# Joined gate and up matmuls: a copy moved ahead of a high part on ScalarE, an add moved ahead of a low part on VectorE

## The chip, the cores and the metric

The kernel runs on one core of a Trainium2 chip, in one launch. The metric is the device time of the whole program in microseconds (us). The kernel before takes 2538.83 us, the median of three runs (2538.58 to 2539.39).

## The reference

Two transformer blocks, one behind the other, over 512 tokens of width 1024 in float32. The change touches only the four gated nets ("nets 0 to 3") of the first block, two in each of its two layers:

```python
def swiglu(h, w_gate, w_up, w_down):
    return (jax.nn.silu(h @ w_gate) * (h @ w_up)) @ w_down

for l in range(DEPTH):                                   # DEPTH = 2
    x = x + 0.5 * swiglu(rms_norm(x, ffn1_norm[l]), ffn1_wg[l], ffn1_wu[l], ffn1_wd[l])
    ...                                                  # attention and short convolution
    x = x + 0.5 * swiglu(rms_norm(x, ffn2_norm[l]), ffn2_wg[l], ffn2_wu[l], ffn2_wd[l])
```

The hidden width is 2816, which is 22 tiles of 128. The second block (convolution, latent attention, cross attention, an MLP of width 4096) is not touched.

## The kernel before

**Split numbers.** Matmuls are made in float32r. Each operand is held as a high part (a rounded copy, made by ScalarE: `..._hi`) and a low part (the rest, made by VectorE as value minus high part: `..._lo`).

**Activations and weights.** Weights come from HBM through a ring of four slots of `raw` (SyncE's queue), 8 tiles of 128x128 to a slot.

**The nets.** Each net takes its 22 hidden tiles in two ways. The first 6 (net 0) or 4 (nets 1 to 3) go in pairs (`pair`): gate and up product apart. The others, 16 or 18 to a net and 70 in all, go one to a window (`fast_window`), where gate and up product of a tile are joined in a scheme of sums (seven products where the plain one has eight): 7 calls of `terms`, each of 4 pairs of matmuls (128x512 and 128x256 columns), write into `bank[0]`, `psT` and `bank[1]`. Partial results are copied out of `bank[0]` three and a half times by ScalarE (L1695, L1704, L1708, L1717) and added by VectorE (L2423, L2433, L2439, L2448, L2450). Two more additions are done by accumulating DMAs that GpSimd issues (L3345 into `tmp[0]`, L3348 into `tmp[2]`). VectorE scales both (L2442, L2453), ScalarE takes the silu (L1723), VectorE multiplies (L2456), and the hidden tile is split (`hidden_hi` L1687, `hidden_lo` L2410).

**Side products.** Between these calls TensorE multiplies tiles of an earlier group of hidden tiles with down weights into `psS` (`side(w, 0)` and `side(w, 1)`, 3 to 5 tiles each, 3 matmuls a tile); `side_adds` adds finished chunks to `x`. The low parts of these down weights are made by `whole_hi` (ScalarE writes the high part and the negated raw value's copy, L1629 and L1630) and another accumulating DMA of GpSimd (`side_lo`, L3337).

**Weights of the next window.** While window w runs, VectorE and ScalarE make those of window w+1: `corner_hi` and `corner_lo` (`cwh`, `cwl`), `weight_sums` (L2322, L2325, L2327), `sums_hi` and `sums_lo` in two halves (L1622, L2333), `last_hi` and `last_lo` (L1637, L2338).

**What sets the order.** All orders are written out by hand: each engine does its own list in that order, and semaphores hold it where it needs another. SyncE's queue loads, for each window, gate weights (L579), up weights (L579), and two units of down weights (L603, one or two pieces each). The gate slot and the second down slot come free at the end of `weight_sums`, the up slot and the first down slot at the end of `last_lo`. The down loads also wait for the accumulating DMA that read their slot before. The order of each engine's list inside `fast_window` is what is changed. TensorE's list (`fast_window` at L921) stays; its waits `k_sn` are ScalarE's copies, `k_ev` VectorE's adds, `k_lo` VectorE's low parts. GpSimd's list is

```python
pool.wait_ge(k_ev, 5 * g + 1)                    # L2423
pool.dma_start(tmp[0][:, 0:QT], tmp[1][:, 0:QT], accum_op=ALU.add).then_inc(k_fd[0], 16)
side_lo(g, 1, net.side_cols(w, 1))               # waits for whole_hi(w, 1)
pool.wait_ge(k_ev, 5 * g + 2)                    # L2433
pool.dma_start(tmp[2][:, QT:S], tmp[3][:, QT:S], accum_op=ALU.add).then_inc(k_fd[1], 16)
```

Of the kernel before, what the change touches and what calls it, by code (L numbers as in the profile page):

```python
# [40 lines left out]
def build(nc, t, out):  # L41
# [75 lines left out]
    with ctx:  # L117
# [217 lines left out]
        s_h = sem("hidden_ready")  # L335
# [1239 lines left out]
        def _(act):  # L1575
# [22 lines left out]
            def ffn(c0, q0, N, nf):  # L1598
# [25 lines left out]
                def whole_hi(j, i):  # L1624
                    c = c0 + 4 * (PLAIN + j)
                    landing(c + 2 + i)
                    act.wait_ge(s_used, q0 + c - RING + 2 + 2 * i)
                    a, b_, n = (2 * i + 1) * UNIT, (2 + i) * UNIT, side_cols(j, i)
                    act.activation(whi[:, a:a + n], raw[:, b_:b_ + n], ACT.Copy).then_inc(s_hi, 1)  # L1629
                    act.activation(wlo[:, a:a + n], raw[:, b_:b_ + n], ACT.Copy, scale=-1.0).then_inc(k_nh, 1)  # L1630
# [53 lines left out]
                def hidden_hi(w):  # L1684
                    tile = 2 * PLAIN + w
                    act.wait_ge(s_h, fb + tile + 1)
                    act.activation(chunk(hhi, tile % HT), tmp[3 if w < 0 else 2][:, :], ACT.Copy).then_inc(s_hh, 1)  # L1687

                def fast_window(w):
                    u, g, f = 4 * (PLAIN + w), G0 + w, fb + 2 * PLAIN + w  # L1690
                    on = w + 1 < FAST
                    act.wait_ge(k_pe, 5 * g + 1)
                    if g:
                        act.wait_ge(k_ev, 5 * g - 4)
                    act.activation(part[0][:, :], bank[0][:, :], ACT.Copy).then_inc(k_sn, 1)  # L1695
                    if w == 0:
                        hidden_hi(-1)
                    whole_hi(w, 1)
                    if on:
                        corner_hi(w + 1)  # L1700
                    act.wait_ge(k_pe, 5 * g + 3)
                    if g:
                        act.wait_ge(k_ev, 5 * g)
                    act.activation(part[2][:, :], bank[0][:, :], ACT.Copy).then_inc(k_sn, 1)  # L1704
                    act.wait_ge(k_pe, 5 * g + 4)
                    if g:
                        act.wait_ge(k_ev, 5 * g - 2)
                    act.activation(part[1][:, :], bank[0][:, :], ACT.Copy).then_inc(k_sn, 1)  # L1708
                    if on:
                        sums_hi(w + 1, 0)  # L1710
                        whole_hi(w + 1, 0)
                    else:
                        ahead(u + 4)
                        ahead(u + 5)
                    act.wait_ge(s_used, q0 + c0 + u + 3)
                    act.wait_ge(k_ev, 5 * g + 2)
                    act.activation(part[1][:, 0:QT], bank[0][:, QT:S], ACT.Copy).then_inc(k_sn, 1)  # L1717
                    if on:
                        sums_hi(w + 1, 1)
                    else:  # L1720
                        ahead(u + 6)
                    act.wait_ge(s_gs, f + 1)
                    act.activation(tmp[0][:, :], tmp[0][:, :], ACT.Silu).then_inc(s_si, 1)  # L1723
                    if on:
                        last_hi(w + 1)
                    hidden_hi(w)

                for w in range(PLAIN):
                    pair(w)
                for w in range(FAST):  # L1730
                    fast_window(w)
                for m in range(KC):
                    ahead(LAST_AT + m + AHEAD)
                    x_hi(N + 1, m)
                    if m == 0:
                        act.activation(acc[:, :], chunk(x, m), ACT.Square).then_inc(s_sq, 1)
                        continue
                    if m > 2:
                        act.wait_ge(s_sq, (N + 1) * KC + m - 1)
                    act.activation(tmp[m % 2][:, :], chunk(x, m), ACT.Square).then_inc(s_sqm, 1)  # L1740
# [523 lines left out]
        def _(dve):  # L2264
# [35 lines left out]
            def ffn(c0, q0, N, nf):  # L2300
# [29 lines left out]
                def sums_lo(j, i):  # L2330
                    dve.wait_ge(s_hi, q0 + c0 + 4 * (PLAIN + j) + 1 + 2 * i)
                    a = 2 * i * UNIT
                    dve.tensor_tensor(wlo[:, a:a + UNIT], tw[:, i * UNIT:(i + 1) * UNIT], whi[:, a:a + UNIT].bitcast(F32),  # L2333
                                      ALU.subtract).then_inc(k_lo, 1)
# [5 lines left out]
                def ahead(u):  # L2340
                    if u == 4 * PLAIN:
                        sums_lo(0, 0)
                    elif u == 4 * PLAIN + 1:
                        pass
                    elif u == 4 * PLAIN + 2:
                        sums_lo(0, 1)
                        last_lo(0)
                    else:
                        split(c0 + u, q0, UNIT_TILES.get(u, 8), 2 if u == LAST_AT else 1)
# [49 lines left out]
                def side_adds(w, i):  # L2399
                    ends = side_ends(w, i)  # L2400
                    if ends:
                        dve.wait_ge(s_used, q0 + c0 + 4 * (PLAIN + w) + 2 + 2 * i)
                    for grp, m in ends:
                        dve.scalar_tensor_tensor(chunk(x, m), psS[:, m % 2 * S:(m % 2 + 1) * S], 0.5, chunk(x, m), ALU.mult,
                                                 ALU.add).then_inc(k_xa, 1)
# [7 lines left out]
                def fast_window(w):  # L2413
                    u, g, f = 4 * (PLAIN + w), G0 + w, fb + 2 * PLAIN + w
                    c = q0 + c0 + u
                    on = w + 1 < FAST
                    t1, t2 = quarter
                    split1 = lambda j, t: folds(tmps[:, j * S:(j + 2) * S])[:, :, t]
                    if w:
                        side_adds(w - 1, 1)  # L2420
                    dve.wait_ge(k_pe, 5 * g + 2)
                    dve.wait_ge(k_sn, 4 * g + 1)
                    dve.tensor_tensor(split1(0, t1), folds(psT[:, 0:S]), folds(part[0][:, :]), ALU.add).then_inc(k_ev, 1)  # L2423
                    if on:
                        corner_lo(w + 1)
                        weight_sums(w + 1)
                        sums_lo(w + 1, 0)
                    else:
                        ahead(u + 4)
                    dve.wait_ge(k_pe, 5 * g + 4)  # L2430
                    dve.wait_ge(k_sn, 4 * g + 3)
                    dve.wait_ge(s_hl, f)
                    dve.tensor_tensor(split1(2, t2), folds(bank[1][:, :]), folds(part[1][:, :]), ALU.add).then_inc(k_ev, 1)  # L2433
                    side_adds(w, 0)
                    if not on:
                        ahead(u + 5)
                    dve.wait_ge(s_used, c + 3)
                    dve.wait_ge(k_sn, 4 * g + 4)
                    dve.tensor_tensor(tmp[0][:, t2], bank[0][:, 0:QT], part[1][:, t1], ALU.add).then_inc(k_ev, 1)  # L2439
                    dve.wait_ge(k_ev, 5 * g + 3)  # L2440
                    dve.wait_ge(k_fd[0], 16 * (g + 1))
                    dve.tensor_tensor(tmp[0][:, :], tmp[0][:, :], inv[:, :], ALU.mult).then_inc(s_gs, 1)  # L2442
                    if on:
                        sums_lo(w + 1, 1)
                    else:
                        ahead(u + 6)
                    dve.wait_ge(k_pe, 5 * g + 5)
                    dve.tensor_tensor(part[2][:, :], bank[1][:, :], part[2][:, :], ALU.add).then_inc(k_ev, 1)  # L2448
                    dve.wait_ge(k_ev, 5 * g + 4)
                    dve.tensor_tensor(tmp[2][:, t1], part[2][:, t1], part[2][:, t2], ALU.add).then_inc(k_ev, 1)  # L2450
                    dve.wait_ge(k_ev, 5 * g + 5)
                    dve.wait_ge(k_fd[1], 16 * (g + 1))
                    dve.tensor_tensor(tmp[2][:, :], tmp[2][:, :], inv[:, :], ALU.mult).then_inc(s_us, 1)  # L2453
                    dve.wait_ge(s_us, f + 1)
                    dve.wait_ge(s_si, f + 1)
                    dve.tensor_tensor(tmp[2][:, :], tmp[2][:, :], tmp[0][:, :], ALU.mult).then_inc(s_h, 1)  # L2456
                    if on:
                        last_lo(w + 1)
                    hidden_lo(w)

                for w in range(PLAIN):
                    pair(w)
                for w in range(FAST):
                    fast_window(w)
                side_adds(FAST - 1, 1)
                for m in range(KC):
                    ahead(LAST_AT + m + AHEAD)
# [973 lines left out]
```

## Time and profile before

| | |
|---|---|
| median of three runs | 2538.83 us |
| profiled execution, its own time | 2540.39 us |
| its span, first to last instruction | 2538.5 us |
| TensorE matmul busy | 2496.1 us (98%) |
| VectorE busy | 2021.7 us (80%) |
| ScalarE busy | 1371.9 us (54%) |
| GpSimd busy | 551.5 us (22%) |
| granted TensorE clock | 1.000 |

The profile is of one execution. PE is TensorE, DVE VectorE, ACT ScalarE, POOL GpSimd, SP SyncE. Times in a row are from the start of the span. The end of a matmul is modelled, so the distance from the start of one to the start of the next says more than its duration. The windows lie from 79 to 333 us (net 0), 577 to 850 (net 1), 932 to 1205 (net 2) and 1454 to 1730 (net 3).

### The profile page before, as it was taken

How to read it: one execution, taken by the hardware profiler on the slowest of the kernel's cores; microseconds unless marked ns; L12 is line 12 of the kernel's file. 1: busy time of each engine (PE TensorE's matmuls, PEld its weight loads, DVE VectorE, ACT ScalarE, POOL GpSimd, SP SyncE). 2: the span in 40 equal slices, each digit the busy share in tenths (PEclk: the TensorE clock that was granted, in tenths of full speed). 3: DMA queues.
4: the chain of work that ended last, by engine and by line, in shares of the span. 5: the costliest groups of instructions: out<-in, count | busy, mean ns of one | idle time of the engine just before them, and what ended most of it. 6: DMA issues, size and time to landing. Idle time of an engine off the chain costs nothing.

```text
span 2538.5 us, 33440 instructions
## 1 busy us (share of the span) xinstructions
PE 2496.1 (98%) x12252; PEld 2079.6 (82%) x12252; DVE 2021.7 (80%) x2760; ACT 1371.9 (54%) x2185; POOL 551.5 (22%) x530
## 2 busy tenths in 40 slices
PE   9999999999999999999999999999999999999999
PEld 7888888888878888888888878788888888888887
DVE  7788877778888688888677788886899787788873
ACT  5555545446555465555454555554578535655442
POOL 4122201322222002222023122221078322100002
PEclk9999999999999999999999999999999999999999
DMA  5566642235656536666422266665333333333331
GB/s 158 132 148 148 144 114 86 80 90 134 144 139 149 135 89 147 142 152 148 113 67 87 84 141 139 142 150 142 96 79 77 118 98 108 87 102 105 101 104 58
DMA packets 527608, 296.99 MB, mean 117 GB/s; under 512 B 46801, under 2 KB 516566, under 8 KB 527190
## 3 DMA queue, kind: packets, MB, share of 16 engines
q1 hardware_dynamic: 486674, 244.19, 33.3%
q0 software_dynamic: 40320, 50.35, 12.0%
q8 instruction: 98, 1.61, 0.3%
q14 instruction: 64, 0.52, 0.1%
q10 hardware_dynamic: 452, 0.32, 0.0%
HBM read 240.27 MB, written 4.19 MB: 96 GB/s over the span
## 4 chain that ended last, share of the span: by engine, by line
PE 68%; DVE 14%; DMA 8%; ACT 5%; issue 4%; POOL 0%; DVEq 0%; ACTq 0%
PE bank L893 6%; PE bank L776 6%; PE bank L777 6%; PE bank L778 6%; DMA raw<-in_ffn_wu 5%; DMA tmps<-tmps 3%; PE bank L894 3%; PE bank L1455 3%; DVE tw L2322 2%; PE psT L958 2%; PE psT L959 2%; PE psT L960 2%; ACT whi L1622 2%; PE psS L914 2%; PE psS L916 2%
## 5 line engine op out<-in xcount | busy, mean ns | idle before, releaser
L2269 DVE TENSOR_TENSOR wlo<-raw,whi 128x1024 fp32r<-128x1024 f32 (+2 forms) x212 | 288.9, 1364 | 51.7 <-ACT whi L1582 48.4
L893 PE MATMUL bank<-xshl,whi 128*128 128x512 f32 x840 | 302.8, 402 | 15.7 <-ACT part L1695 14.4
L776 PE MATMUL bank<-xhl,whi 128*128 128x512 f32 x672 | 264.5, 394 | 0.0
L777 PE MATMUL bank<-xhl,whi 128*128 128x512 f32 x672 | 261.9, 390 | 0.0
L778 PE MATMUL bank<-xhl,wlo 128*128 128x512 f32 x672 | 261.8, 390 | 0.0
L894 PE MATMUL bank<-xshl,wlo 128*128 128x256 f32 x840 | 235.5, 280 | 0.0
L1582 ACT ACTIVATE whi<-raw 128x1024 fp32r<-128x1024 f32 (+2 forms) x209 | 214.4, 1029 | 34.3 <-PE bank L778 21.9
L893 PEld LDWEIGHTS bank<-xshl,whi 128*128 128x128 f32 x840 | 157.6, 188 | 66.7 <-issue 30.7
L3337 POOL DMA_DIRECT2D wlo<-raw x140 | 167.1, 1194 | 177.4 <-ACT wlo L1630 177.4
L914 PE MATMUL psS<-hhi,whi 128*128 128x512 f32 x488 | 192.2, 394 | 0.0
L916 PE MATMUL psS<-hhi,wlo 128*128 128x512 f32 x488 | 191.2, 392 | 0.0
L915 PE MATMUL psS<-hlo,whi 128*128 128x512 f32 x488 | 190.8, 391 | 0.0
L2333 DVE TENSOR_TENSOR wlo<-tw,whi 128x1024 fp32r<-128x1024 f32 x140 | 171.0, 1221 | 24.6 <-ACT whi L1622 24.6
L1622 ACT ACTIVATE whi<-tw 128x1024 fp32r<-128x1024 f32 x140 | 147.9, 1057 | 24.1 <-DVE tw L2325 23.2
L3345 POOL DMA_DIRECT2D tmps<-tmps x70 | 60.5, 865 | 456.7 <-DVE tmps L2423 456.7
L894 PEld LDWEIGHTS bank<-xshl,wlo 128*128 128x128 f32 x840 | 158.6, 189 | 0.0
L1687 ACT ACTIVATE hhi<-tmps 128x512 fp32r<-128x512 f32 x74 | 46.8, 633 | 200.3 <-DVE tmps L2456 197.6
L778 PEld LDWEIGHTS bank<-xhl,wlo 128*128 128x128 f32 x672 | 126.2, 188 | 26.7
L776 PEld LDWEIGHTS bank<-xhl,whi 128*128 128x128 f32 x672 | 126.2, 188 | 26.5 <-issue 1.1
L777 PEld LDWEIGHTS bank<-xhl,whi 128*128 128x128 f32 x672 | 126.3, 188 | 26.1 <-issue 1.0
L3348 POOL DMA_DIRECT2D tmps<-tmps x70 | 60.6, 866 | 375.3 <-DVE tmps L2433 375.3
L1708 ACT ACTIVATE part<-bank 128x512 f32<-128x512 f32 x70 | 41.9, 599 | 152.3 <-PE bank L894 152.3
(698 smaller groups left out, 6967.9 us busy)
## 6 DMA issues: line engine op xcount, KB each, us to landing
raw<-in_ffn_wg SPq DMA_DIRECT2D x88, 512.0 KB
raw<-in_ffn_wu SPq DMA_DIRECT2D x88, 512.0 KB
raw<-in_w_in SPq DMA_DIRECT2D x53, 512.0 KB
raw<-in_w_mlp SPq DMA_DIRECT2D x40, 512.0 KB
tmps<-tmps POOLq DMA_DIRECT2D x140, 128.0 KB, 3.2
wlo<-raw POOLq DMA_DIRECT2D x80, 192.0 KB, 3.7
wlo<-raw POOLq DMA_DIRECT2D x52, 256.0 KB, 4.3
raw<-in_ffn_wd SPq DMA_DIRECT2D x48, 256.0 KB
```

The source lines that it names most:

```text
L776: pe.matmul(dest, a, rhs_hi(k), start=start and k == 0, stop=False)
L777: pe.matmul(dest, a, rhs_lo(k), start=False, stop=False)
L778: mm = pe.matmul(dest, b_, rhs_hi(k), start=False, stop=stop and k == tiles - 1)
L893: pe.matmul(folds(dest), a, mhl, start=start and k == 0, stop=False, skip_group_check=True)
L894: mm = pe.matmul(dest[:, 0:QT], b_, mh, start=False, stop=stop and k == 3, skip_group_check=True)
L914: pe.matmul(dest, whi[:, a:a + P], chunk(hhi, at_h), start=k == 0, stop=False)
L915: pe.matmul(dest, whi[:, a:a + P], chunk(hlo, at_h), start=False, stop=False)
L916: mm = pe.matmul(dest, wlo[:, a:a + P], chunk(hhi, at_h), start=False, stop=last)
L1582: act.activation(whi[:, a:a + n], raw[:, a:a + n], ACT.Copy).then_inc(s_hi, 1)
L1622: act.activation(whi[:, 2 * i * UNIT:(2 * i + 1) * UNIT], tw[:, i * UNIT:(i + 1) * UNIT], ACT.Copy).then_inc(s_hi, 1)
L2269: dve.tensor_tensor(wlo[:, a:a + n], raw[:, a:a + n], whi[:, a:a + n].bitcast(F32), ALU.subtract).then_inc(s_split, units)
L2333: dve.tensor_tensor(wlo[:, a:a + UNIT], tw[:, i * UNIT:(i + 1) * UNIT], whi[:, a:a + UNIT].bitcast(F32), ALU.subtract).then_inc(k_lo, 1)
```

## The change

On ScalarE, `hidden_hi` of a window's tile goes from the end of its own window to behind the first copy (L1695) of the next, and `whole_hi(w, 1)` goes from behind the first copy to behind the second (L1704). On VectorE, the first up quarter (L2433) goes ahead of `sums_lo(w+1, 0)`; `sums_lo(w+1, 1)` goes from behind L2442 to behind the product L2456, ahead of `last_lo`; `hidden_lo` of a tile goes from the end of its window to behind L2423 of the next, which gets a wait for the product (`s_h`). After the last window of a net both halves of the hidden tile are made behind the loop. In that window the split of the third unit of the last down product (`ahead(u + 6)`) goes to behind the product.

```diff
@@ ScalarE, fast_window
                     act.activation(part[0][:, :], bank[0][:, :], ACT.Copy).then_inc(k_sn, 1)
-                    if w == 0:
-                        hidden_hi(-1)
-                    whole_hi(w, 1)
+                    hidden_hi(w - 1)
                     if on:
                         corner_hi(w + 1)
...
                     act.activation(part[2][:, :], bank[0][:, :], ACT.Copy).then_inc(k_sn, 1)
+                    whole_hi(w, 1)
                     act.wait_ge(k_pe, 5 * g + 4)
...
                     if on:
                         last_hi(w + 1)
-                    hidden_hi(w)
...
                 for w in range(FAST):
                     fast_window(w)
+                hidden_hi(FAST - 1)
@@ VectorE, fast_window
                     dve.wait_ge(k_sn, 4 * g + 1)
+                    dve.wait_ge(s_h, f)
                     dve.tensor_tensor(split1(0, t1), folds(psT[:, 0:S]), folds(part[0][:, :]), ALU.add).then_inc(k_ev, 1)
+                    if w:
+                        hidden_lo(w - 1)
                     if on:
                         corner_lo(w + 1)
                         weight_sums(w + 1)
-                        sums_lo(w + 1, 0)
                     else:
                         ahead(u + 4)
...
                     dve.tensor_tensor(split1(2, t2), folds(bank[1][:, :]), folds(part[1][:, :]), ALU.add).then_inc(k_ev, 1)
+                    if on:
+                        sums_lo(w + 1, 0)
                     side_adds(w, 0)
...
                     dve.tensor_tensor(tmp[0][:, :], tmp[0][:, :], inv[:, :], ALU.mult).then_inc(s_gs, 1)
-                    if on:
-                        sums_lo(w + 1, 1)
-                    else:
-                        ahead(u + 6)
                     dve.wait_ge(k_pe, 5 * g + 5)
...
                     dve.tensor_tensor(tmp[2][:, :], tmp[2][:, :], tmp[0][:, :], ALU.mult).then_inc(s_h, 1)
                     if on:
+                        sums_lo(w + 1, 1)
                         last_lo(w + 1)
-                    hidden_lo(w)
+                    else:
+                        ahead(u + 6)
...
                 for w in range(FAST):
                     fast_window(w)
+                hidden_lo(FAST - 1)
                 side_adds(FAST - 1, 1)
```

## Rows read from the trace of the kernel before

**Rows 1.** Waits of TensorE, whole span: us in total, times, longest.
```profile
PE bank L893 <- ACT part L1695: 14.4, 31, 1.2
PE bank L893 <- DVE tmps L2433: 12.2, 32, 0.7
```

**Rows 2.** Chain that ended last, 620 to 655: start us, us, what.
```profile
624.08 3.75 DMA raw<-in_ffn_wu
...
632.08 0.68 DVE tmps L2433
...
634.49 1.13 DVE wlo L2333
635.62 0.61 DVE part L2448
...
636.72 0.70 DVE tmps L2453
...
638.77 4.10 DMA raw<-in_ffn_wu
...
642.89 1.24 DVE tw L2322
...
647.12 0.69 DVE tmps L2433
...
648.20 3.84 DMA tmps<-tmps
...
652.12 0.70 DVE tmps L2453
```

**Rows 3.** Executions of L2433, nets 1, 2, 3: ns min/median/max, first and last start.
```profile
L2433 DVE TENSOR_TENSOR tmps<-bank,part x17: 680/683/685, 587.4 to 830.0; 128x512 f32<-128x512 f32 x17
...
L2433 DVE TENSOR_TENSOR tmps<-bank,part x17: 680/683/685, 943.0 to 1185.7; 128x512 f32<-128x512 f32 x17
...
L2433 DVE TENSOR_TENSOR tmps<-bank,part x17: 680/683/684, 1464.6 to 1710.6; 128x512 f32<-128x512 f32 x17
```

**Rows 4.** Timeline, TensorE: a tile of a side product, a pair of a set.
```profile
301.14 0.40 PE L914 MATMUL psS<-hhi,whi 128*128 128x512 f32 x1
...
301.83 0.39 PE L914 MATMUL psS<-hhi,whi 128*128 128x512 f32 x1
...
303.53 0.40 PE L893 MATMUL bank<-xhl,cwh 128*128 128x512 f32 x1
...
303.88 0.40 PE L893 MATMUL bank<-xhl,cwh 128*128 128x512 f32 x1
```

**Rows 5.** Timeline, VectorE.
```profile
304.20 0.69 DVE L2456 TENSOR_TENSOR tmps<-tmps 128x512 f32<-128x512 f32 x1
304.81 0.69 DVE L2338 TENSOR_TENSOR dwl<-raw,dwh 128x512 fp32r<-128x512 f32 x1
...
644.95 0.69 DVE L2327 TENSOR_TENSOR tw<-raw,tw 128x512 f32<-128x512 f32 x1
```

**Rows 6.** DMA of L3348, all 70, one, and chain pieces; SyncE's gate loads.
```profile
DMA to landing us min/median/max: 2.7/3.3/6.1
...
631.07 0.50 SPq L579 DMA_DIRECT2D raw<-in_ffn_wg  x1
633.15 0.86 POOL L3348 DMA_DIRECT2D tmps<-tmps  x1 [5.67 <-DVE tmps L2433]
DMA to landing us min/median/max: 2.7/2.7/2.7
...
1109.81 0.42 SPq L579 DMA_DIRECT2D raw<-in_ffn_wg  x1
1110.40 3.99 DMA tmps<-tmps
...
1571.77 0.42 SPq L579 DMA_DIRECT2D raw<-in_ffn_wg  x1
1571.89 4.87 DMA tmps<-tmps
```

## The prediction

> **What bounds the kernel now.** Read the page's busy times first, then TensorE's waits, then the chain of waits over a few windows; the order matters, because the first view misleads. TensorE is busy 98% of the span (the table of the profile before), which suggests that only its waits can be won. In the 70 joined windows it waits at two places: for ScalarE's first copy (L1695, 14.4 us) and for VectorE's first up quarter (L2433, 12.2 us) [rows 1]. The edit aims at both. But the chain of waits inside a net does not run through TensorE. It is a closed loop, once round per window: first up quarter L2433; GpSimd's adding DMA into `tmp[2]`; L2453; the product L2456; the low part L2338 (`last_lo`), which frees the slot of raw up weights; the load of the next up weights; their sums L2322 to L2327; ScalarE's high part; the low part `sums_lo(.,0)`; and L2433 again [rows 2]. From 632.08 to 647.12 that is 15.04 us. Over the 48 turns of nets 1 to 3 (three times 16, from 17 executions each) it takes (242.6 + 242.7 + 246.0) / 48 = 15.23 us [rows 3].
>
> TensorE alone needs less. A window has 28 pairs of matmuls for the gate and up product at 0.35 us and on average 120 / 18 = 6.7 tiles of the down product at 0.69 us [rows 4]: 9.8 + 4.6 = 14.4 us. So in nets 1 to 3 TensorE waits because the loop is 0.8 us longer. What the edit does to the loop decides, not what it does to one wait.
>
> **The loop, link by link, before.** From the start of L2433 to GpSimd's issue 1.08 us; the DMA lands; 0.08 us to L2453 (652.12 against 648.20 + 3.84) [rows 2]. If the DMA lands soon, VectorE's own work holds L2453 instead: 636.72 - 632.08 = 4.64 us. From L2453 to the issue of the up load 638.77 - 636.72 = 2.05; load to L2322 4.12 here, and 3.75 for the load of the turn before [rows 2]: 3.95, between them (either end moves the sum by 48 x 0.2, 10 us). L2322 to L2433 647.12 - 642.89 = 4.23. The mean turn then leaves 15.23 - 2.05 - 3.95 - 4.23 = 5.0 for L2433 to L2453.
>
> **What the edit takes out.** L2433 goes ahead of `sums_lo(w+1,0)`, so it no longer waits for ScalarE's high part and the low part. L2322 to L2327 is 644.95 - 642.89 = 2.06 us [rows 2, 5], and an independent instruction starts 0.61 behind one of this size (L2338 behind L2456) [rows 5]: 2.67 instead of 4.23, so 1.56 less. L2433 also waits for the third gate sum and ScalarE's copy of it. From one L2433 to that sum TensorE has six sets of four pairs (8.4 us), 3.3 tiles (2.3) and 0.8 us at the start by the order of the code, 11.5 in all, and the copy 0.6: 12.1, some 3 us ahead of the next L2433.
>
> **What it puts in.** `sums_lo(w+1,1)` moves from before the wait for the second up sum to between the product and `last_lo`. It takes 635.62 - 634.49 = 1.13 us [rows 2]. It used to fill part of the 4.64, beside the DMA; now it stands whole in front of the load of the up weights. If ScalarE's high part for it were late it would cost more, but that copy needs only the weight sums and the last gate set, both done before L2439. So L2453 to the load is 2.05 + 1.13 = 3.18.
>
> These two alone give -1.56 + 1.13 = -0.43 a turn. VectorE's work between L2433 and L2453 stays about the same (`sums_lo(.,0)` comes in, `sums_lo(.,1)` goes), 4.64 at most with no wait for a copy in it, which a landing above 3.5 exceeds. Then the DMA path decides: turn = 1.08 + landing + 0.08 + 3.18 + 3.95 + 2.67 = 10.96 + landing. It breaks even with 15.23 at a landing of 4.27 us.
>
> **The landing is the step that turns the sign.** The end of L2327 also frees the slot of raw gate weights, and SyncE issues their 512 KB at once. Today L2433 comes late enough that the adding DMA goes out 2.08 us after the gate load (631.07 and 633.15) and lands in 2.7 [rows 6]. Where it goes out 0.59 us behind (1109.81, 1110.40) it lands in 4.0, and 0.12 behind (1571.77, 1571.89) in 4.9 [rows 6]: gate load and adding DMA finish in the order of their issue. The edit brings L2433 1.56 us nearer to the gate load: 2.08 - 1.56 = 0.5 us behind where the slot loads have one piece, about 0 where SyncE first issues two pieces of down weights or waits for an accumulating DMA of low weights. By those two rows that is 4.1 and 5.0. Weighing them about half and half, 4.6. Bounds: 2.7 (no collision) and 6.1, the longest of all [rows 6]. The turn becomes 10.96 + 4.6 = 15.56: +0.33 us, times 48 = +16 us.
>
> The Trainium skill speaks against this reading: "DMA: Bandwidth & Descriptors", section "Queues, rings and completion order", has each DMA engine take turns between queues packet by packet, so a small DMA would not stand behind a large one. By that rule the landing would stay near its median 3.3 and the kernel would be faster. The rows above show the small one landing later the closer it follows; I go by them.
>
> **The other edits.** `hidden_hi` behind L1695: L1695 no longer stands behind a copy that waits for the product, so TensorE's 14.4 us there go; since the loop sets the turn, they reappear in the wait for L2433. Taken at nothing. If the loop were shorter than TensorE, up to 14.4 us would be real. `whole_hi(w,1)` behind the second copy: its adding DMA stands on GpSimd behind the one for `tmp[0]`, which waits for L2423, so it goes out about as before; a delay would hold the down load of SyncE's queue and the gate load behind it, and that would push the collision, not TensorE. `hidden_lo(w-1)` behind L2423: one 0.61 us spacing moved within VectorE, in the 3.95 us in which it waits for the up load (side add, L2423, `hidden_lo` at 0.61 each and the low part of `cwl` at 1.13: 3.0, so 0.9 of cover). Side products read a new hidden tile at the earliest as fourth tile of a group, some 2 us after their start, itself behind five sets of matmuls. The new wait of L2423 for the product is on VectorE's own earlier instruction: zero; behind it stands only L2423, for which GpSimd's first adding DMA waits. In the last window the split of a down unit now precedes the last low part by about 1 us, under the 12 tiles x 0.69 = 8.3 us of `last_down` that do not need it. `hidden_hi(FAST - 1)` keeps its place.
>
> Entry: the first L2433 of each net has no loop behind it and comes earlier, bounded by TensorE's own pace, about 0.7 us for each of three nets (the longest wait of this kind [rows 1]): -2 us. Net 0 has 8 tiles a window (15.3 us of TensorE, up to 16.7 in its first windows): loop and TensorE are near each other, before and after; 0, within 5 either way.
>
> **Sum.** The profiled execution took 2540.39 us outside (span 2538.5), the median is 2538.83. 2540.4 + 16 - 2 = 2554.4, less the 1.6 by which the profiled one is above the median: 2553 us.
>
> **Rivals.**
> (a) Faster: the adding DMA does not queue behind the gate load, or only for half. With a landing of 3.3 the loop is 14.26 and TensorE's 14.4 decides: -0.8 x 48 = -40, with 5 from net 0 and entry: 2495. With 3.8: 14.76, 48 x -0.47 = -23: 2516 or so. For it: after 2.08 us nothing is left of the collision, and both PE waits are real. Against: the two close pairs. It decides from a landing below 4.2. It is what the rule named above would bring.
> (b) No change: landings of 4.2 to 4.4, turn within 0.1 of today's: 2539 within 5.
> (c) Clearly slower: the gate load goes out with the adding DMA in nearly every window, and the landing is 5.3: 16.26, +1.03 x 48 = +49: 2586. Also the up load could lengthen, since GpSimd's first adding DMA now follows it one 0.61 us instruction sooner; 0.3 us would be +14.
> (d) TensorE is the bound after all and the edit takes out its two waits: 26.6 us less, 2512. Against: after either wait it is not TensorE that the chain returns to [rows 2]. Counted with (a).
>
> **How the numbers follow.** Forecast (landing 4.4 to 5.0, 2545 to 2575) 0.48; (c) 0.09; (b) 0.15; (a) with (d) 0.28. Less than 0.2% (5 us) can't be told from no change. So faster 0.28, same 0.15, slower 0.57. The forecast's own range is 2545 to 2575; for 8 in 10 it reaches from 2505, inside (a), to 2582.
>
> **What would show it.** L2322 to L2433 2.7 us instead of 4.2; L2453 to the up load 3.2 instead of 2.05; landing of L3348's DMA (the same statement after) 4.6 in the median instead of 3.3, its issue 0 to 0.6 us behind the gate load; TensorE no longer waiting for L1695's copy and more for L2433's sum (over 0.5 us a window in nets 1 to 3). The prediction is wrong if the landing stays under 4, or if L2433 starts on something other than the end of the weight sums, for instance the copy of the third quarter.

## The result and the profile after

The changed kernel takes 2560.62 us (median of four runs, 2558.68 to 2564.60), the kernel before in the same set 2539.11 us. The ratio is 1.0086, 95% interval 1.0068 to 1.0103: 22 us slower. The forecast was 2553 us, slower. Of the two waits of TensorE that the edit aims at, one goes and the other grows to four times its length.

Two words are used throughout. A turn is the time from one start of the first up quarter to the next, once round the loop. The landing of a DMA is the time from the start of its issue to the end of its transfer.

TensorE's waits after, whole span (us in total, times, longest). The wait for L1695 is gone, that for the first up quarter (now L2434) is four times what it was [rows 1]; L1702 is the second copy, L1704 before:

```profile
PE bank L893 <- DVE tmps L2434: 50.0, 40, 2.2
...
PE bank L893 <- ACT part L1702: 1.3, 2, 1.0
```

The first up quarter's executions in nets 1, 2 and 3, as [rows 3] (ns min/median/max, first and last start). The 48 turns take (253.2 + 255.3 + 253.3) / 48 = 15.87 us each, where they took 15.23:

```profile
L2434 DVE TENSOR_TENSOR tmps<-bank,part x17: 683/684/686, 581.4 to 834.6; 128x512 f32<-128x512 f32 x17
...
L2434 DVE TENSOR_TENSOR tmps<-bank,part x17: 683/685/685, 945.5 to 1200.8; 128x512 f32<-128x512 f32 x17
...
L2434 DVE TENSOR_TENSOR tmps<-bank,part x17: 683/685/687, 1477.7 to 1731.0; 128x512 f32<-128x512 f32 x17
```

One turn of the chain that ended last, 628 to 646, as [rows 2] (start us, us, what; L2321 = L2322 before, L2452 = L2453, L2332 = L2333, L2337 = L2338):

```profile
629.67 0.69 DVE tmps L2434
...
630.75 4.82 DMA tmps<-tmps
...
635.66 0.70 DVE tmps L2452
...
637.00 0.17 DVE wlo L2332
...
638.13 0.70 DVE dwl L2337
...
638.85 3.87 DMA raw<-in_ffn_wu
...
642.75 1.24 DVE tw L2321
...
645.41 0.70 DVE tmps L2434
```

The reader is to see three things. From L2321 to L2434 it is 645.41 - 642.75 = 2.66 us, where 4.23 was. From L2452 to the up load it is 3.19, where 2.05 was, with the low part L2332 now in between. And the adding DMA takes 4.82 us.

A landing of that length is the median now. The DMA of L3350 (L3348 before [rows 6]), all 70:

```profile
DMA to landing us min/median/max: 2.8/4.8/7.0
```

The issues of the gate load (SyncE) and of the adding DMA (GpSimd) in two neighbouring windows, from the timeline:

```profile
630.22 0.50 SPq L579 DMA_DIRECT2D raw<-in_ffn_wg  x1
630.75 0.86 POOL L3350 DMA_DIRECT2D tmps<-tmps  x1 [5.12 <-DVE tmps L2434]
...
646.49 0.87 POOL L3350 DMA_DIRECT2D tmps<-tmps  x1 [4.40 <-DVE tmps L2434]
647.76 0.45 SPq L579 DMA_DIRECT2D raw<-in_ffn_wg  x1
```

The landing of the second of them alone:

```profile
DMA to landing us min/median/max: 3.3/3.3/3.3
```

In the first the gate load goes out 0.53 us ahead of the adding DMA, which lands in 4.8. In the second SyncE was held up and the gate load follows 1.27 us behind; the adding DMA lands in 3.3, and that turn takes 660.05 - 645.41 = 14.6 us. The gate load is not alone. SyncE issues the second down load of the window, 192 to 256 KB in one or two pieces, 0.4 to 1.0 us ahead of it (here at 629.78). Where the text says gate load, this down load goes with it.

### The profile page after: what moved, and what is told of

Same layout as the page of the kernel before. It is cut to its first block, busy times and chain, and to the rows that moved or that the text cites. A ratio compares the mean times of both kernels' runs of the same rounds, so it can differ in the third digit from the quotient of the medians.

```text
span 2560.7 us, 33440 instructions
## 1 busy us (share of the span) xinstructions
PE 2495.8 (97%) x12252; PEld 2086.3 (81%) x12252; DVE 2001.0 (78%) x2760; ACT 1367.9 (53%) x2185; POOL 549.6 (21%) x530
## 4 chain that ended last, share of the span: by engine, by line
PE 59%; DMA 17%; DVE 14%; issue 6%; ACT 3%; DVEq 0%; POOL 0%; ACTq 0%
DMA tmps<-tmps 9%; DMA raw<-in_ffn_wu 8%; PE bank L776 5%; PE bank L777 5%; PE bank L778 5%; PE bank L893 4%; DVE tw L2321 3%; PE bank L1455 3%; PE bank L894 2%; DVE tw L2324 2%; PE psT L958 2%; PE psT L959 2%; PE psT L960 2%; DVE tmps L2434 2%; PE psT L776 2%
## 5 line engine op out<-in xcount | busy, mean ns | idle before, releaser
L3339 POOL DMA_DIRECT2D wlo<-raw x140 | 146.4, 1045 | 223.5 <-ACT wlo L1630 222.7
L3347 POOL DMA_DIRECT2D tmps<-tmps x70 | 60.4, 863 | 524.8 <-DVE tmps L2423 524.8
L2332 DVE TENSOR_TENSOR wlo<-tw,whi 128x1024 fp32r<-128x1024 f32 x140 | 170.5, 1218 | 2.0 <-ACT whi L1622 1.6
L893 PE MATMUL bank<-xshl,dwh 128*128 128x512 f32 x280 | 107.9, 418 | 50.0 <-DVE tmps L2434 50.0
L2321 DVE TENSOR_TENSOR tw<-raw 128x1024 f32<-128x1024 f32 x70 | 85.7, 1225 | 74.4 <-DMA raw<-in_ffn_wu 74.4
L2452 DVE TENSOR_TENSOR tmps<-tmps,inv 128x512 f32<-128x512 f32 x70 | 48.5, 693 | 95.3 <-DMA tmps<-tmps 94.8
```

Of the source, the lines that this page charges most:

```text
L893: pe.matmul(folds(dest), a, mhl, start=start and k == 0, stop=False, skip_group_check=True)
L2321: dve.tensor_tensor(tw[:, S:3 * S].rearrange("p (u n) -> p u n", u=2), raw[:, UNIT:2 * UNIT].rearrange("p (u n) -> p u n", u=2), first, AL ...
```

## The experiments

All edits are in the four nets alone. The links in the texts are means over the 48 turns of nets 1 to 3 in the profiled execution. They run between the starts of the first up quarter, of the product with `inv` that waits for the adding DMA (L2453 before), of the up load's issue and of the first weight sum.

**e1: the up slot freed first.**

```diff
                     if on:
+                        last_lo(w + 1)
                         sums_lo(w + 1, 1)
-                        last_lo(w + 1)
...
                     if j == 0:
                         dve.wait_ge(s_ro, 13)
+                    if g:
+                        dve.wait_ge(k_lo, 3 * g)     # in weight_sums: the low parts that read tw are done
```

> The changed kernel with last_lo(w+1) ahead of sums_lo(w+1,1), so that the up slot is freed 1.13 us sooner (and a wait on the low parts in weight_sums, long fulfilled, to keep tw safe). Theory (the turn is the loop through the adding DMA and the up load): L2452's counterpart to the up load 3.2 -> 2.05 us, landing of the adding DMA stays near 4.8 us, turn 15.9 -> 14.75 us, which is close to TensorE's own 14.4: 48 x -1.1 = -53 us against the changed kernel, about 2508 us, so faster than both. Rival (TensorE or VectorE's total work sets the turn): the moved low part costs VectorE the same wherever it stands, so nothing changes, 2556 to 2565 us.

Measured: 2502.62 us, ratio 0.9852 (0.9836 to 0.9869). Turn 14.68 us, landing 4.6 on average. The same arithmetic instructions on the same engine in a different order (with one wait added that is long fulfilled) are worth 58 us against the changed kernel. One turn, as before, 606 to 620; after the product only `last_lo` stands before the load:

```profile
607.39 0.69 DVE tmps L2436
...
608.47 4.87 DMA tmps<-tmps
...
613.43 0.70 DVE tmps L2454
...
614.77 0.70 DVE dwl L2339
...
615.48 3.93 DMA raw<-in_ffn_wu
...
619.43 1.24 DVE tw L2323
```

The rival, that VectorE's total work or TensorE's pace set the turn, falls.

**e2: the gate load held back.** On SyncE, ahead of the second down load of a window, behind which the next gate load stands:

```diff
                     if w:
                         sp.wait_ge(k_sl[i], 16 * (net.first_g + w))
+                    if w and i:
+                        sp.wait_ge(k_fd[1], 16 * (net.first_g + w))
```

> The changed kernel, where SyncE holds the second down load and the gate load behind it until the adding DMA into tmp[2] has landed (one wait more on its queue). Theory (the adding DMA lands late because the gate load is in front of it): landing 4.8 -> 2.8 us, loop 11.0 + 2.8 = 13.8 us, so TensorE's 14.4 decides: 48 x -1.4 = -67 us, about 2494 to 2505 us; if the gate load then runs into the up load behind it, up to 1 us of that comes back in the up load's transit, 2545 us. Rival (the adding DMA is slow of itself in its new place, for instance by GpSimd's descriptors written while VectorE works, or by the low weights' DMA beside it): the landing stays at 4.5 to 4.8 us and the time at 2556 to 2565 us.

Measured: 2500.66 us, ratio 0.9849 (0.9834 to 0.9864). Landing, all 70:

```profile
DMA to landing us min/median/max: 2.7/2.7/6.1
```

VectorE's order is that of the changed kernel; the second down load and the gate load behind it are later, the gate load on average 3.5 us behind the adding DMA. The median landing goes from 4.8 to 2.7, the turn from 15.87 to 14.68. So it was these loads that the adding DMA waited for. The hold moves both; no run tells the share of the smaller down load from that of the gate load.

**e3: the hidden halves moved alone**, from the kernel before.

```diff
-                    if w == 0:
-                        hidden_hi(-1)
+                    hidden_hi(w - 1)
                     whole_hi(w, 1)
...
-                    hidden_hi(w)
...
+                    dve.wait_ge(s_h, f)
                     dve.tensor_tensor(split1(0, t1), ...)
+                    if w:
+                        hidden_lo(w - 1)
...
-                    hidden_lo(w)
```

> The kernel before with one part of the change alone: hidden_hi behind the first copy L1695 of the next window on ScalarE, hidden_lo behind L2423 of the next window on VectorE, with the wait for the product. Theory (loop): TensorE's 14.4 us of waits for L1695 go, the turn stays 15.2 us, the wait turns up at the first up quarter (12 -> about 25 us); 2535 to 2541 us, no change; a gain of 2 to 4 us in the entries of the nets at most. Rival (TensorE's waits count): 2525 us.

Measured: 2535.69 us, ratio 0.9990 (0.9980 to 0.9999). TensorE's wait for L1695 is gone and its wait for the first up quarter (L2435) takes it over, against [rows 1]:

```profile
PE bank L893 <- DVE tmps L2435: 27.7, 36, 1.8
```

A wait of 14.4 us was removed, and another grew by 15.5 us. The turn is 15.23, as before.

**e4: the first up quarter ahead of the first low part alone**, from the kernel before.

```diff
                         weight_sums(w + 1)
-                        sums_lo(w + 1, 0)
...
                     dve.tensor_tensor(split1(2, t2), ...)
+                    if on:
+                        sums_lo(w + 1, 0)
```

> The kernel before with the other part alone: the first up quarter ahead of sums_lo(w+1,0), while sums_lo(w+1,1) stays where it was. Theory (loop): L2322 to the first up quarter 4.23 -> 2.67 us; the adding DMA goes out behind the gate load by 0.5 us or less and lands in about 4.8 us; from the first up quarter to L2453 6.0 us by the DMA or 5.8 by VectorE's work, which now has both low parts in it; then 2.05 and 4.0: turn 14.7 us, 48 x -0.5 = -25 us: 2512 us (2505 to 2525). So the loss of the change is the other low part's new place, together with the collision. Rival (the collision alone makes the change slow, the place of the low part does not matter): 2555 us. Rival (TensorE's waits are what counts): -12 us, 2527 us.

Measured: 2523.04 us, ratio 0.9937 (0.9922 to 0.9951): faster, as the loop says and against its first rival, but 11 us less so than expected. The second rival, 2527 us by TensorE's waits, is only 4 us away, and this run alone does not exclude it; e3 does. The turn is 14.96, not 14.7: first up quarter to L2453's counterpart (L2454) takes 6.3 us where the landing explains 5.9. VectorE's own work is not longer than counted, 647.68 - 641.82 = 5.86 us where it waits for nothing. What comes on top is a wait for ScalarE's last copy (L1717). TensorE's and VectorE's waits, whole span, then the chain from 662:

```profile
PE bank L893 <- ACT part L1695: 17.5, 43, 1.7
...
DVE tmps L2440 <- ACT part L1717: 45.6, 57, 1.9
```

```profile
662.58 0.70 DVE tmps L2454
663.31 0.70 DVE tmps L2457
...
664.57 0.59 ACT part L1695
665.30 0.47 PE bank L893
```

So this kernel has a second loop, now about as long as the first. The product (L2457) releases `hidden_hi`, behind which ScalarE makes L1695; TensorE waits for L1695, and all that TensorE and ScalarE do in that window comes later, the copy of L1717 too.

**e5: the changed kernel with one edit undone**, `sums_lo(w + 1, 1)` back ahead of the wait for the second up sum.

```diff
                     dve.tensor_tensor(tmp[0][:, :], tmp[0][:, :], inv[:, :], ALU.mult).then_inc(s_gs, 1)
+                    if on:
+                        sums_lo(w + 1, 1)
+                    else:
+                        ahead(u + 6)
...
-                        sums_lo(w + 1, 1)
                         last_lo(w + 1)
-                    else:
-                        ahead(u + 6)
```

> The changed kernel with one edit undone: sums_lo(w+1,1) (in the last window ahead(u+6)) is back behind the product with inv, ahead of the wait for the second up sum. Loop theory: the adding DMA still collides with the gate load (landing 4.8 us), first up quarter to L2453's counterpart 6.0 to 6.3 us (VectorE's own work is now as long as the DMA's path), then 2.05, 4.0 and 2.67: turn 14.7 to 15.0 us; 2502 to 2520 us. So this one edit is what made the change slow. Rival (the collision alone is enough): 2550 us or more.

Measured: 2503.40 us, ratio 0.9862 (0.9846 to 0.9877). The landing is still 4.7 us in the median, the turn 14.66. So against the changed kernel this one edit is worth 57 us.

The comparison with e4 shows one thing more. This kernel is e4's with the hidden halves moved (and `whole_hi`), which makes L1695 independent of the product: TensorE's 17.5 us of waits for L1695 are gone, VectorE's wait for the last copy falls from 45.6 to 21.2 us, and the time from 2523 to 2503. The edit that was worth 3 us in e3 is worth some 20 here, because here the loop through the adding DMA is no longer the only one that counts. (`whole_hi` moved with it; no run moves the hidden halves alone here.)

**e6: the changed kernel with `whole_hi(w, 1)` back behind `hidden_hi`.**

```diff
                     hidden_hi(w - 1)
+                    whole_hi(w, 1)
...
-                    whole_hi(w, 1)
```

> The changed kernel with the other ScalarE edit undone: whole_hi(w,1) is back ahead of corner_hi and the second copy. Loop theory: ScalarE is not in the loop, GpSimd's DMA of these low parts waits for the one into tmp[0] anyway; the same as the changed kernel within 5 us, 2555 to 2566 us; if the low weights land sooner, the gate load goes out sooner and the landing is 0.1 us shorter: 2555 us. Rival (ScalarE's copies delay the loop): the early place takes ScalarE's time before cwh, 2570 us or more.

Measured: 2558.66 us, ratio 1.0085 (1.0067 to 1.0104), no difference from the changed kernel that the intervals can tell (the profiled turn is 15.69). Inside, TensorE's waits change place: 14.7 us for the second copy instead of 1.3, 29.5 us for the first up quarter instead of 50.0.

**e7: the hold of e2 in the kernel before.**

```diff
+                    if w and i:
+                        sp.wait_ge(k_fd[1], 16 * (net.first_g + w))
```

> The kernel before with the hold alone: SyncE keeps the second down load and the gate load until the adding DMA into tmp[2] has landed. Loop theory: landing 3.4 -> 2.8 us, first up quarter to L2453 5.0 -> 4.7 us; the up load goes out only about 2.8 us behind the gate load and may take 0.2 to 0.3 us more, as it did by 0.15 in e2: 48 x (-0.3 to 0) us, 2524 to 2540 us. Rival (the hold by itself, not the collision that it ends, makes the gain of e2): 2500 us.

Measured: 2582.91 us, ratio 1.0172 (1.0157 to 1.0188). A miss: I expected 2524 to 2540. The adding DMA lands in 2.7 us in the median, as expected. But in this kernel the up load goes out so soon that the held gate load is only 2.4 us ahead of it in the median, where it was 7.7. At the closest it is 1.1 us. SyncE's issues, then the chain, around 664:

```profile
663.90 0.42 SPq L579 DMA_DIRECT2D raw<-in_ffn_wg  x1
665.01 0.39 SPq L579 DMA_DIRECT2D raw<-in_ffn_wu  x1
```

```profile
664.30 0.70 DVE dwl L2340
...
665.01 6.14 DMA raw<-in_ffn_wu
...
671.18 1.24 DVE tw L2324
```

The up load, 1.1 us behind the gate load, takes 6.1 us where it took 3.75 to 4.1 [rows 2]; over all turns 4.9. The collision was moved from one DMA of the loop to the other: 0.74 us a turn, 36 us, and net 0 is 7 us longer as well. In e2 the up load goes out 1.0 us later in the turn (the low part stands before it), 3.4 us behind the gate load, and there it took 4.2.

**e8: e1 and e2 together**, both diffs above on the changed kernel:

```diff
+                        sp.wait_ge(k_fd[1], 16 * (net.first_g + w))
...
+                        last_lo(w + 1)
                         sums_lo(w + 1, 1)
-                        last_lo(w + 1)
```

> e1 and e2 together: last_lo ahead of sums_lo(w+1,1), and the gate load held until the adding DMA has landed. Loop theory: the loop would be 4.6 + 2.05 + 4.2 + 2.67 = 13.5 us, far under TensorE's pace, of which e1 and e2 show 14.68 with hardly a wait left; so little more than e1's and e2's last waits: 2496 to 2501 us, the fastest of all. Rival (there is no floor by TensorE there, the two gains add): 2460 us.

Measured: 2496.73 us, ratio 0.9835 (0.9820 to 0.9850).

**e9: the second low part in its new place alone**, from the kernel before: e5's edit the other way round.

```diff
-                    if on:
-                        sums_lo(w + 1, 1)
-                    else:
-                        ahead(u + 6)
                     dve.wait_ge(k_pe, 5 * g + 5)
...
                     if on:
+                        sums_lo(w + 1, 1)
                         last_lo(w + 1)
+                    else:
+                        ahead(u + 6)
                     hidden_lo(w)
```

> The kernel before with one edit of the change alone: sums_lo(w+1,1) (in the last window ahead(u+6)) between the product and last_lo. Loop theory: the gate load is still about 1.7 us ahead of the adding DMA, landing 3.4 us, so first up quarter to L2453's counterpart 1.16 + 3.4 = 4.6 us (5.0 before, since VectorE's 4.64 floor is gone), then 3.18, 3.95 and 4.23: turn 15.96 us, 48 x +0.73 = +35 us: 2574 us (2565 to 2583). The edit is slow by itself, and slower than the whole change. Rival (it is slow only together with the collision): 2539 to 2545 us.

Measured: 2579.11 us, ratio 1.0163 (1.0146 to 1.0180). The turn is 15.86, with 4.5 for first up quarter to L2453, 3.18, 3.96 and 4.22.

**e10: e8's kernel again, in more rounds.**

> The fastest kernel so far (last_lo ahead of sums_lo(w+1,1), gate load held until the adding DMA has landed) once more, in five rounds, for its ratio to the kernel before: 0.983 to 0.984, 2496 to 2498 us.

Measured: 2495.99 us, ratio 0.9834 (0.9819 to 0.9848): the fastest kernel of this study, 43 us under the kernel before.

The turns of all of them, in us; each row's four links add up to its turn within 0.1. The median times also hold net 0 and the entries of the nets, so equal turns need not mean equal times:

```
kernel                          quarter->product  ->up load  ->weight sum  ->quarter   turn   median time
before                                5.01          2.05        3.94         4.23     15.23   2539
changed                               5.98          3.18        4.04         2.67     15.87   2561
e6  changed, whole_hi back            5.91          3.18        3.93         2.67     15.69   2559
e9  low part moved alone              4.50          3.18        3.96         4.22     15.86   2579
e7  gate load held, before            4.80          2.05        4.90         4.23     15.97   2583
e3  hidden halves alone               5.04          2.05        3.92         4.22     15.23   2536
e4  quarter ahead alone               6.32          2.05        3.92         2.67     14.96   2523
e5  changed, low part back            6.06          2.05        3.88         2.67     14.66   2503
e1  changed, last_lo first            5.95          2.05        4.01         2.67     14.68   2503
e2  changed, gate load held           4.64          3.18        4.19         2.67     14.68   2501
e8  e1 and e2                         5.31          2.05        4.46         2.68     14.51   2497
e10 e8's kernel again                 5.45          2.05        4.32         2.68     14.50   2496
```

The last five stand at or near TensorE's own pace: it is busy 251.84 of 252 us from 580 to 832 in e8 (250.9 to 251.8 in e1, e2 and e5), and 237.53 in the changed kernel (columns: stretch, length, then busy us and instructions of PE, PEld, DVE, ACT, POOL, clock, DMA share, GB/s). First e8, then the changed kernel:

```profile
580.00:832.00 252.00, 251.84 (x1317) 213.46 (x1316) 217.64 (x297) 149.84 (x241) 59.27 (x69) 1.00 0.67 154
```

```profile
580.00:832.00 252.00, 237.53 (x1222) 199.12 (x1221) 201.95 (x277) 138.03 (x225) 55.98 (x65) 0.99 0.60 140
```

## Why the prediction was right, step by step

**The loop decides, not TensorE's waits: right.** e3 removes a wait of 14.4 us for 3 us of gain. The turns account for most of every difference above; e1 differs from the changed kernel only in the order of two low parts. What the turns leave is net 0 and the entries: e9 and the changed kernel have the same turn and lie 18 us apart, because e9's net 0 is longer and its entries gain nothing.

**First up quarter ahead, -1.56 us: right**, 2.67 us in all kernels that have the edit.

**Low part ahead of `last_lo`, +1.13: right**, 3.18 in all that have it. e9 shows it alone: it costs 40 us. The expectation had 2574. The turns brought less than expected, 0.63 x 48 = 30 us for 35, and net 0, which I had left out, more: from its first to its last first-up-quarter (334.7 - 90.9) - (328.3 - 91.0) = 6.5 us more than before. Together they are the 36.9 us by which the profiled spans differ.

**Collision with the gate load: right in kind, a little small.** I took 4.6 us; the mean over the 48 turns is 4.79, worth 0.19 x 48 = 9 us. By distance, in the changed kernel: the gate load 0.3 to 0.7 us ahead, 19 windows, mean 4.6 us; within 0.3, 26 windows, 5.2; 0.3 or more behind, 13 windows, 3.5. (Four more have it 0.71 us ahead, mean 4.3; eight have none near.) I had weighed the first two classes half and half and had no row for the third. I had also named the gate load alone, where the second down load goes out just ahead of it. e2 takes both away and gets the price back.

**Up load 3.95: small by 0.09**, 4 us.

**Net 0 and the entries: too small.** I gave 0 and -2 us. From the last first-up-quarter of a net to the first of the next it is 2.07 us less in each case (257.05 after net 0 against 259.12), 6.2 in sum, and net 0's last one is 4.0 us earlier (324.34 against 328.32). The bound was mine: I limited the entry by TensorE's wait there. But the first up quarter itself comes 2.07 us sooner (1.56, and about 0.5 because `cwh` is ready sooner: L2314 waited 0.49 us for it at the entry of net 2 and no longer does), and where the loop is slower than TensorE it is the loop's start that counts. The sum then closes: 48 x 0.64 = 31 from the turns, 1.6 from the last interval of net 3, less 6.2 and 4.0, gives 22; the spans differ by 2560.7 - 2538.5 = 22.2.

**The clock: not in the forecast, small.** In the changed kernel TensorE's granted clock falls to 1.2 GHz, half of 2.4, for 3.4 us at a time in four places (from 695, 1155, 1637 and 1732), each time right behind a wait of 1.9 to 2.1 us for the first up quarter. In the kernel before it stays up through the nets. The fourth falls into the last interval of net 3, where no up load is waited for: 16.4 us, where the same interval of nets 1 and 2 is 14.85. That is the 1.6 above. The other three fall into turns that the loop sets (15.98, 15.33 and 15.87 us against a mean of 15.87), and these are no longer than the rest.

**ScalarE's two edits at nothing: right** (e3, e6), as long as the loop is longer than TensorE. The prediction said that TensorE's waits for L1695 would be real if it were not, and e4 against e5 is that case: some 20 us.

**TensorE's own pace 14.4: nearly**; 14.51 in e8.

**Rivals.** (a), no queueing behind the gate load, is refuted by e2 and by the distances; (d), TensorE as the bound, by e3. (c), a landing of 5.3, did not come about, though one turn in seven is at 5.4 or more. What the forecast missed is how much depended on one edit: with the low part left where it was (e5) the same collision is there and the kernel is 1.4% faster than before. Neither the collision (e5) nor the low part (e2) alone makes a slow kernel here; only together do they lift the loop above TensorE's pace. From the kernel before, where the loop is already above it, the low part alone does (e9).

## What to carry to other kernels

When the chain of waits closes on itself once per iteration, write the loop down link by link, DMAs included, and judge an edit by what it does to the sum; an engine with 98% busy time and a few visible waits then only follows the loop. That holds for the one kernel: an edit that gave 3 us while the loop was the longer one gave some 20 once it was not (e3, then e4 to e5), so try such edits again after the loop has been shortened. In such a loop the instruction that frees a slot for the next load goes first, and low parts that nobody needs for several us go behind it. When a small transfer on the loop moves, look at which large ones go out in the 2 us ahead of it: holding a load that has slack can be worth more than any reordering, as long as it is not pushed in front of another transfer of the loop.

## What the runs showed of the hardware

A small accumulating DMA (128 KB, GpSimd's queue) near 704 to 768 KB of loads from HBM on SyncE's queue (a down load of 192 to 256 KB and, 0.4 to 1.0 us behind it, the gate load of 512 KB) was slow to land. It took 4.6 us on average when issued 0.3 to 0.7 us behind the gate load, 5.2 within 0.3 us of it on either side, and 2.7 in the median when the loads were held. When the gate load went out 0.3 us or more later, it mattered less (3.5). The trace's own records of the packets show that the delay comes before the transfer: the first packet of the adding DMA starts 1.4 us after its issue with the loads held (e2), 3.15 us after it when it is issued within 0.3 us of the gate load, and 2.6 us at 0.3 to 0.7 (means).

The Trainium skill, "DMA: Bandwidth & Descriptors", section "Queues, rings and completion order", describes engines that take turns between queues packet by packet. These distances look like order of arrival instead, and the measurement decides here. Which part of the path makes that order, the runs don't tell.

Two loads on one queue did the same to each other. In e7, with the down load and the gate load ahead of them, eleven up loads went out 1.1 to 1.6 us behind the gate load and took 5.0 to 6.2 us; in the kernel before, 7.7 us behind it in the median, they took 3.9 on average.
